# A two-block transformer kernel in split fp32: joint products taken out of ga to co, rows of 2,304 bytes for the first activation buffer, and waits of TensorE for its own last product at four panels

## The reference, cut to what matters

```python
# first block
a = rms_norm(h, norm_mix)
qkv = a @ w_qkv                                  # 2048 x 6144, then stick-breaking attention (16 heads)
h = h + o @ w_o                                  # 2048 x 2048
h = h + square(relu(rms_norm(h, norm_mlp) @ w1)) @ w2   # 2048 x 8192, 8192 x 2048
h = rms_norm(h, final_norm)
# second block: 16 meta tokens stand ahead of the 256 tokens
hn = rms_norm_2(h, norm_mix_g)
u, gb_in, gc_in, v_in, ga_lin, gbr_lin = split(hn @ w_in)          # 2048 x 12288
y_a = pool(u) @ pool_w * pool_scale              # trailing means over 2, 4, 8, 16 tokens
y_b = (gb_in * causal_conv3(gc_in * v_in)) @ conv_out_w
h = h + (sigmoid(ga) * y_a + sigmoid(gbr) * y_b) @ w_o2
h = h + (silu(hn2 @ w_gate) * (hn2 @ w_up)) @ w_down               # 2048 x 11264, 5632 x 2048
out = rms_norm_2(h, norm_final_g)[:, 16:]
```

## Time and profile before

| | |
|---|---|
| Three runs | 2572.61, 2572.88 (median), 2573.26 us |
| The profiled execution | 2572.07 us, span of its instructions 2570.3 us, granted clock 0.999 |
| PE busy | 2561.2 us (100%), 19,871 matmuls |
| PEld busy | 2461.8 us (96%) |
| DVE, ACT, POOL busy | 1578.9, 1153.0, 139.1 us (61%, 45%, 5%) |
| DMA | 485.64 MB, mean 189 GB/s, 56.8% of 16 engines |

### The profile page before, as it was taken

How to read it: one execution, slowest core, us unless ns; L and a number is a source line. 1 busy time by engine, 2 the same in 40 slices (tenths; PEclk the granted TensorE clock), 3 DMA queues, 4 the chain that set the end, 5 groups by cost and what they waited for, 6 DMA issues and landing times.

```text
span 2570.3 us, 47399 instructions
## 1 busy us (share of the span) xinstructions
PE 2561.2 (100%) x19871; PEld 2461.8 (96%) x19871; DVE 1578.9 (61%) x1343; ACT 1153.0 (45%) x1126; POOL 139.1 (5%) x87
## 2 busy tenths in 40 slices
PE   9999999999999999999999999999999999999998
PEld 9999999999999999999899988899999889998997
DVE  6577766655556556786654776566755555555555
ACT  5455554434434434544533344444444434443444
POOL 0000100000000000000200530000000000000001
PEclk9999999999999999999999999999999999999999
DMA  7554455556555565555555555555555556555563
GB/s 263 184 165 163 164 181 188 192 195 196 195 190 191 195 197 196 186 181 189 183 186 188 183 181 195 182 195 197 193 187 193 182 195 197 196 190 190 194 212 131
DMA packets 243978, 485.64 MB, mean 189 GB/s; under 512 B 7729, under 2 KB 8945, under 8 KB 243697
## 3 DMA queue, kind: packets, MB, share of 16 engines
q1 hardware_dynamic: 243520, 483.12, 56.8%
q10 hardware_dynamic: 320, 0.53, 0.1%
HBM read 481.53 MB, written 2.10 MB: 188 GB/s over the span
## 4 chain that ended last, share of the span: by engine, by line
PE 99%; DVE 0%; POOL 0%; issue 0%; ACT 0%; DVEq 0%; POOLq 0%; ACTq 0%
PE ps L1414 48%; PE ps L1422 24%; PE ps L1385 8%; PE ps L1347 8%; PE ps L1391 4%; PE ps L1357 4%; PE ps L1470 0%; PE ps L1524 0%; PE ps L1436 0%; PE ps L1458 0%; PE ps L1407 0%; PE ps L1278 0%; PE ps L1288 0%; PE ps L1529 0%; PE ps L1507 0%; PE ps L1461 0%
## 5 line engine op out<-in xcount | busy, mean ns | idle before, releaser
L790 DVE TENSOR_TENSOR wlo<-raw,whi 128x1024 fp32r<-128x1024 f32 x900 | 1138.9, 1274 | 944.1 <-ACT whi L582 943.8
L582 ACT ACTIVATE whi<-raw 128x1024 fp32r<-128x1024 f32 x900 | 949.9, 1060 | 1335.9 <-PE ps L1422 1008.4
L1414 PE MATMUL ps<-b_buf,whi 128*128 128x256 f32 x5734 | 711.5, 276 | 0.5 <-DVE za L1005 0.5
L1414 PEld LDWEIGHTS ps<-b_buf,whi 128*128 128x128 f32 x5734 | 679.6, 188 | 1.1 <-DVE za L1005 0.7
L1422 PE MATMUL ps<-b_buf,wlo 128*128 128x256 f32 x2880 | 386.3, 276 | 0.0
L1422 PEld LDWEIGHTS ps<-b_buf,wlo 128*128 128x128 f32 x2880 | 354.4, 188 | 0.0
L1414 PE MATMUL ps<-a_buf,whi 128*128 128x258 f32 (+4 forms) x2560 | 330.9, 282 | 0.0
L1414 PEld LDWEIGHTS ps<-a_buf,whi 128*128 128x128 f32 x2560 | 315.7, 188 | 0.3
L1414 PE MATMUL ps<-c_buf,whi 128*128 128x256 f32 x2542 | 314.4, 276 | 0.0
L1414 PEld LDWEIGHTS ps<-c_buf,whi 128*128 128x128 f32 x2542 | 300.4, 188 | 0.2
L1347 PE MATMUL ps<-a_buf,whi 128*128 128x512 f32 x768 | 185.7, 394 | 0.0
(11 more groups left out here) (206 smaller groups left out, 1254.4 us busy)
## 6 DMA issues: line engine op xcount, KB each, us to landing
raw<-in_mlp_w_dram SPq DMA_DIRECT2D x128, 1024.0 KB, 5.4
raw<-in_w_in_dram SPq DMA_DIRECT2D x96, 1024.0 KB, 5.1
raw<-in_w_gate_up_dram SPq DMA_DIRECT2D x88, 1024.0 KB, 5.0
raw<-in_sb_w_qkv_dram SPq DMA_DIRECT2D x44, 1024.0 KB, 5.1
raw<-in_w_down_dram SPq DMA_DIRECT2D x44, 1024.0 KB, 5.0
raw<-in_sb_w_o_dram SPq DMA_DIRECT2D x16, 1024.0 KB, 5.0
raw<-in_conv_out_w_dram SPq DMA_DIRECT2D x16, 1024.0 KB, 5.0
raw<-in_w_o_dram SPq DMA_DIRECT2D x16, 1024.0 KB, 5.0
```

Of the source, the lines that this page charges most:

```text
L582: act.activation(whi[:, unit_of(n, u)], raw[:, n % RAW, u * UK:(u + 1) * UK, :], ACT.Copy).then_inc(w_hi, 1)
L790: dve.tensor_tensor(wlo[:, s], raw[:, n % RAW, u * UK:(u + 1) * UK, :], cast(whi[:, s]), ALU.subtract).then_inc(w_lo, 1)
L1414: pe.matmul(outs[j], whi[:, s, kt, j * P:(j + 1) * P], part[:, x, tok], start=first and kt == 0 and part is hi and (alone or j % 2 == 0), ...
```

## The change

- An A row becomes 576 columns (2,304 bytes): 16 meta, 256 tokens high, 256 tokens low, the meta tokens' low part in reversed order, 32 unused. High and low tokens of a tile now lie 1,024 bytes apart. `ms` moves into space that is free at the time.
- `paired_chunk` and `RUNS` go; ga, gb, gbr and co run through `chunk`, 192 products of 256 columns a panel. ga and gb are written out as four panels.
- `Panel` has `joint`, a number of joint products for each chunk, and `settle`, by which PE waits before the panel's first product until its own last product has counted `w_used`. Four panels have both, with 5 joint products in chunk 0: q's and w_o's panel 2, ga's and gb's panel 0. In w1_0 the 4 and 5 are replaced by 5 in chunk 3 of panel 0 (behind the norm), in gu_0_first by 5 in chunk 3 of the gate panel; gu_1_first and gu_2_first keep their 4.
- A panel with joint products uses one bank for each j also in q and w_o. There are now 8 such panels where there were 19.
- In the wide kinds the low product takes the low tokens and the reversed meta columns and writes 16 columns further on (`lows`); DVE's evacuation first copies those few columns and adds them where they belong (2 more steps, for 12 panels).

```diff
+ROW = 2 * TW + 32
...
+SETTLED = dict(joint={0: 5}, settle=True)
...
-    add("q", 1, [Panel("q", "w_qkv", 0, lambda i, g=g: g * PW, src="A") for g in range(4)], ("q",))
+    add("q", 1, [Panel("q", "w_qkv", 0, lambda i, g=g: g * PW, src="A", **(SETTLED if g == 2 else {}))
+                   for g in range(4)], ("q",))
...
-            add("w1_0", 1, [Panel("relu2", "w1", 0, lambda i, g=g: g * PW, src="C", needs="w_o", pairs=(4, 5, 0, 0)[g])
+            add("w1_0", 1, [Panel("relu2", "w1", 0, lambda i, g=g: g * PW, src="C", needs="w_o", joint={3: 5} if g == 0 else None)
...
-    loop2("ga", "ga", "w_in", 4 * D, "A", pairs=RUNS)
+    add("ga", 1, [Panel("ga", "w_in", 0, lambda i, g=g: 4 * D + g * PW, src="A", **(SETTLED if g == 0 else {}))
+                  for g in range(4)], ("ga",))
...
-    loop2("gb", "gb", "w_in", 1 * D, "A", pairs=RUNS)
-    loop2("gbr", "gbr", "w_in", 5 * D, "A", pairs=RUNS)
-    add("co", 1, [Panel("co", "conv_out_w", 0, lambda i, g=g: g * PW, src="B", needs="gb", pairs=RUNS if g < 2 else 0)
-                  for g in range(4)], ("co",))
+    add("gb", 1, [Panel("gb", "w_in", 0, lambda i, g=g: 1 * D + g * PW, src="A", **(SETTLED if g == 0 else {}))
+                  for g in range(4)], ("gb",))
+    loop2("gbr", "gbr", "w_in", 5 * D, "A")
+    loop2("co", "co", "conv_out_w", 0, "B", "gb")
...
-        a_buf, a_off = place("a_buf", [P, 2, NT, TW], F32R)
+        a_buf, a_off = place("a_buf", [P, NT, ROW], F32R)
...
+        a_hi, a_lo, b_hi, b_lo = a_buf[:, :, 0:TW], a_buf[:, :, T:2 * TW], b_buf[:, 0], b_buf[:, 1]
+        m_lo = a_buf[:, :, TW + T:2 * TW][:, :, ::-1]
+        a_pair = a_buf[:, :, M:M + 2 * T].rearrange("p t (a n) -> p a t n", a=2)
...
+                if kind in WIDE:
+                    spare = M - WIDE[kind]
+                    step(dve.tensor_copy(S2[:, :, 0:spare], ps[:, 4 * half:4 * half + 4, TW:TW + spare][:, :, ::-1]))
+                    early = ps[:, 4 * half:4 * half + 4, WIDE[kind]:M]
+                    step(dve.tensor_tensor(early, early, S2[:, :, 0:spare], ALU.add))
...
+                if p.settle and c == 0:
+                    pe.wait_ge(w_used, cnt.at("chunk") * UNITS)
...
+                        joint = products[:p.joint.get(c, 0)] if u == 0 else []
...
+                        for part, dst, cols in ((x_hi_, outs, tok), (x_lo_, lows, low_tok)):
```

More of the change, by code:

```diff
@@ L98, with __init__ @@
 class Panel:
-    def __init__(self, kind, weight, row0, col, chunks=CH, tile0=0, src=None, needs=None, pairs=0):
+    def __init__(self, kind, weight, row0, col, chunks=CH, tile0=0, src=None, needs=None, joint=None, settle=False):
         self.kind, self.weight, self.row0, self.col = kind, weight, row0, col
         self.chunks, self.tile0, self.src, self.needs = chunks, tile0, src, needs
-        self.pairs = pairs
+        self.joint, self.settle = joint or {}, settle
+        self.four = kind in FOUR or bool(joint)
     def counts(self):
-        more = TWO_PARTS if self.pairs else {}
+        more = TWO_PARTS if self.joint else {}
         return {k: KINDS[self.kind].get(k, 0) + more.get(k, 0) for k in NAMES}
@@ L209, in make_stages @@
     ready["kv"] = o_ready
-    add("w_o", 1, [Panel("res", "w_o1", 0, lambda i, g=g: g * PW, src="B", needs="kv") for g in range(4)], ("res",))
+    add("w_o", 1, [Panel("res", "w_o1", 0, lambda i, g=g: g * PW, src="B", needs="kv", **(SETTLED if g == 2 else {}))
+                     for g in range(4)], ("res",))
     stages[-1].order = ([(0, 0), (0, 1), (0, 2), (1, 0), (1, 1), (1, 2), (0, 3), (1, 3)] +
@@ L251, in make_stages @@
     for f, n in enumerate((4, 4, 3)):
-        ready[f"gu_{f}"] = (gate_up(f"gu_{f}_first", done, 1, norm=None if f else 2, pairs=(4, 0) if f else (0, 5)) +
+        ready[f"gu_{f}"] = (gate_up(f"gu_{f}_first", done, 1, norm=None if f else 2, joint={0: 4} if f else {3: 5}) +
                             gate_up(f"gu_{f}_rest", done + 1, n - 1, j0=1))
@@ L308, in build @@
         rr1, _ = place("rr1", [P, T])
-        ms, _ = place("ms", [P, 2, TW])
         msum = rr[:, 0:M]
@@ L641, in evac @@
             def evac(p, j):
-                kind, two = p.kind, int(bool(p.pairs))
+                kind, two = p.kind, int(bool(p.joint))
                 dst = {"q": tiles(b_hi, j), "k": k_hi[:], "v": v_hi[:], "res": tiles(c_hi, j),
@@ L1331, in three @@
                 return pe.matmul(out, w_l, x_h, start=False, stop=stop, skip_group_check=True)
[L1333 to L1344, removed]
-                    if back == 0 and kt == 0 and j == 0:
-                        pe.wait_ge(w_hi, cnt.at("chunk") * UNITS + (u + 1))
-                    high = pe.matmul(ps[:, 4 * half + j, :].rearrange("p (a n) -> p a n", a=2),
-                                     whi[:, unit_of(n - back, u), kt, j * P:(j + 1) * P],
-                                     buf[:, :, p.tile0 + (c - back) * KT + u * UK + kt, tok],
-                                     start=i < JT, stop=False, skip_group_check=True)
-                    if back and i % PER_RUN == PER_RUN - 1:
-                        high.then_inc(w_used, 1)
-                for u in range(UNITS):
-                    pe.wait_ge(w_lo, cnt.at("chunk") * UNITS + (u + 1))
-                    for kt in range(UK):
-                        for j in range(JT):
-                            last = pe.matmul(ps[:, 4 * half + j, T:2 * T], wlo[:, unit_of(n, u), kt, j * P:(j + 1) * P],
-                                             buf[:, 0, p.tile0 + c * KT + u * UK + kt, tok], start=False,
-                                             stop=c == p.chunks - 1 and u == UNITS - 1 and kt == UK - 1,
-                                             skip_group_check=True)
-                    if u < UNITS - 1 or end == (c + 1) * PER_RUN:
-                        last.then_inc(w_used, 1)
-                cnt.n["chunk"] += 1
             def chunk(p, c, half):
```

64 lines of the change are left out of this document (29 added, 35 removed).

## The result

Four runs of the changed kernel took 2618.49 to 2619.26 us (median 2618.70), beside 2573.01 for the kernel before: ratio 1.0178 [1.0160, 1.0196]. Forecast were 2559.2 us and a gain of 0.5%; it is 1.8% slower. The profiled execution took 2618.55 us.

What follows compares the result with a forecast made beforehand. PE, busy for the whole span, was taken to bound the kernel. Gains of 13.49 us, settling +1.32 and -0.5, -0.6, -0.4 gave -13.7 from 2572.07; with 0.8 added, 2559.2 us, range 2550 to 2565.

Steps and rivals of the forecast that it cites:

- Two paces that a stream keeps: On PE, 256-column products run at 113.3 or 117.8 ns (21.76 or 22.62 us a panel), and the stream keeps its pace.
- rival 3: The switch to the short pace at gb's start misses, costing 14.4 us up to gu_0's norm; 2573.6 us, chance 0.03.
- The row starts (9 x 256 bytes): A's rows stepping by 9 x 256 bytes look constant to PE, so A holds the short pace as B and C do.
- Rival 4: A cannot hold the short pace, shown by 279 to 283 ns in ga; +9.1 us, 2582 us, chance 0.08.
- five joint products are shown to work from the long pace: Five 512-column products at q, w_o, ga, gb and behind two norms switch PE to the short pace, costing 0.02 us a time.
- A door without a price: Moving joint products behind the norms in w1_0 and gu_0 gains 0.22 us each; no cost of a miss was given.
- rival 2: The switch to the short pace misses at one of q, w_o or ga; 2561.5 to 2563.4 us, chance 0.10.
- Settling: PE's wait for its own last product at q, w_o, ga and gb costs 0.33 us each, 1.32 in all.
- pw: pw's panels go from 22.94 to 21.76 us, gaining 1.18, of which 0.48 is the stall; 0 to 0.5 may return.
- Wide panels: The 258-column products of gc, vv and u stay near today's time on constant rows; -0.5 us taken.
- v: v's first two chunks gain 0.19 us and its other 14 chunks 0 to 1.3, taken as -0.6.
- Rival 5: The pace hangs on neither row starts nor joint products; only split products and settling count, 2578 us, chance 0.02.

Runs made afterwards that it cites:

- experiment 8: Experiment 5 with w1_0's panel 1 and gu_0's up panel entered by 5 joint products without a wait; 2563.91 us, ratio 0.9966.
- experiment 5: Changed kernel with wait plus 4 joint products at q, w_o, gb, w1_0's panel 1 and gu_0's up panel, wait plus 6 at ga; 2597.49 us.
- experiment 6: Experiment 5 with A's rows of 2,176 bytes instead of 2,304; 2615.56 us, ratio 1.0166.
- experiment 4: Changed kernel with the wait kept but no joint products at q, w_o, ga and gb; 2586.48 us, ratio 1.0059.
- experiment 1: Changed kernel with 4 joint products instead of 5 at q, w_o, ga, gb and behind the norms in w1_0 and gu_0; 2583.75 us, ratio 1.0057.
- experiment 9: Experiment 5 with the change's own 5 joint products behind the norms, in place of wait plus 4, in w1_0 and gu_0; 2596.70 us.
- experiment 10: Experiment 5 with 7 joint products instead of 4 at w1_0's panel 1 and 6 at gu_0's up panel, wait kept; 2597.62 us.

## Why the prediction was wrong

**What bounds it, the clock:** right. Nothing but the pace moved more than some 3 us.

**Two paces that a stream keeps:** right, in size as well. The kernel before kept the short one for 674 us, where I had written 640. The eighth experiment's panels take 21.76 us on every stretch that I had named but pw, with 0.1 more in those behind a wait. My price for a miss at gb's door (rival 3, 13.8 us for its 16 panels) measured 13.6 in the change against the forecast (gb and gbr 2.3 + 4.55 - 0.33, the wait's gap ahead of them 0.26, co 2.75 + 0.67, wo2 3.4).

**The row starts (9 x 256 bytes):** right: A holds the short pace in experiments 5 and 8 and loses it in 6. Rival 4, the slower end on which I had put 0.08, is not what happened: A's products showed 279 in ga, which I had named as its sign, but so did B's and C's, and the sign could not tell the rivals apart.

**The step that failed** is the reading of the earlier trace rows: "a few 512-column products ... throw it over", and from that "five joint products are shown to work from the long pace", wherever they stand. What the earlier trace rows shows is one sequence of five, behind single products at the long pace, that ended on 232. Behind a wait the first distance is 313, behind a norm 421; the sequence is shifted, and the fifth falls on 226 or 229. I read one success as a property of the number five. The rows that would have warned me were at hand: the kernel before used 4, 5, 5, 4 and 4, and each of the five sequences ends on 231 or 232.

**A door without a price.** For w1_0 and gu_0 I took 0.22 us each as the whole stake, since the change only moves five joint products from one chunk to the one before. That move puts the norm just ahead of them, and what hangs on them is everything up to the next door: 31 panels x 0.855 = 26.5 us, and 7 panels, 6 us. I priced misses at q, w_o, ga and gb, and not at these two, which made more than half of the error. With a price on them the slower end would have stood at 2592 (both missed), or 2606 with gb's as well. The misses were also not independent, as the chances of rivals 2 and 3 took them: six of six missed, each shifted in the round. Only rival 2's remark that five may throw wrong what the wait has set right touched it, and experiment 4 shows that the wait alone sets nothing right at these four.

**The sum, term by term** (against the forecast of 2558.4 for the profiled execution, 60.2 us): w1_0 to w2_3 27.2, gu_0 with dn_0 6.8, gb to wo2 13.6, ga 3.4, q with k 2.5, w_o 1.9, pw 0.6, v 1.9, wide panels 1.2; together 59.1, the rest in the first panels and between attention's parts. A wait's gap lies in the stretch ahead of its door (0.26 in u for ga's, 0.26 in vv for gb's) and is counted here with the door.
- **Settling**, 0.33 each: in experiment 8 the first panel behind the wait takes 21.86 us instead of 21.76 in q, with about 0.26 of gap ahead of it (380 ns where 118 would stand): 0.36. At w_o, where the last distance is 539, it is 0.5. Right but for w_o.
- **pw**: 22.94 to 22.32, not 21.76; the stall shrank to 0.02 as forecast, and the pace stayed long up to its third panel. In experiment 8, where PE comes sooner, 0.24 of the stall is back (a distance of 356), inside my 0 to 0.5, but it also costs the short pace for two panels (0.43): 22.53 in all. From one stall I had read that a stall throws the stream to the short pace; this one throws it the other way.
- **Wide panels**, -0.5 forecast: gc and vv +0.9 in the change and in experiment 8 (184.15 and 184.16 against 183.25), u +0.3 in both. Without the gaps of the waits it is +0.6 and nothing. Their products' middle duration in gc and vv is unchanged:
```profile
L1394 PE MATMUL ps<-a_buf,whi x1024: 277/282/285, 1334.4 to 1517.2; 128*128 128x258 f32 x171
```
- **v**, -0.6 - 0.19 forecast, the wrong sign: with activations stationary, L1363's products in A take 397 ns in the mean, against 394; the four v panels grew by 1.1 us:
```profile
L1363 PE MATMUL ps<-whi,a_buf 128*128 128x512 f32 x256 | 65.2, 397 | 0.0
```

So the plan, with the doors of experiment 8, was worth 2573 - 2564 = 9 us, not 13.7; between that and the forecast stand wide panels and v (about 3), pw (0.8), the pace behind attention's parts (0.5) and several terms of 0.2: the chunks behind the two norms, w_o's wait.

**Rival 5**, that row starts and joint products set no pace (2578 us), is not what happened: experiment 6 (18 us for 128 bytes a row) and experiment 1 (35 us between the medians for one product fewer at six places) speak against it. The Trainium skill (page "TensorE: Matmul & The Clock Gate", "Step-by-step: what each phase is for") says that weights load through a port of their own and take nothing from the running matmul. These runs contradict what I had drawn from that sentence, that row starts would not matter; whether weight loads take anything they do not show.

**What stays open.** What in PE or its weight loads makes the two paces was not shown. In the trace a weight load of 187 to 188 ns starts 2 to 4 ns behind each product's start at either pace, so these rows don't say which of the two sets it. That the number of joint products decides at one place, and that what works goes with the last distance within a few nanoseconds, is shown; whether that distance is the cause or only a mark of where the stream stands is not, nor why 306 230 236 232 misses and 236 235 232 232 hits. And of experiment 1 only the execution at 2598.92 was traced: which doors fell otherwise in the runs at 2583 and 2608 is not known.

## What to carry to other kernels

Where a dense stream of matmuls can run at two paces, read the pace of every stage (duration of one product, start to start), before and after, even of stages that the change doesn't touch, and price each place that sets the pace by all that runs up to the next such place. A recipe that works in one spot, a count of instructions above all, is a fact of that spot and its entry: when anything ahead of it moves, look at the start-to-start distances there again and choose the count anew. A stall is such a place too: pw's led to either pace. Here other counts at four doors and two doors moved back turned a loss of 1.8% into a gain of 0.34%.

## What the runs showed of the hardware

- Two to seven fp32r products of 512 columns fall into a round of 226, 229, 232 ns between their starts, and their place in it bears on the pace of what follows: all 55 doors that gave the short pace (113.3 ns for 256 columns) ended on a duration of 394 or 395 (24 of them the same two places in twelve kernels), and none of the 29 that ended on another did. Six with 394 did not either.
- In the kernel before the pace then held over 31 panels and 674 us, across changes of buffer and of PSUM banks, up to the first wide product.
- A moving operand whose rows start 2,304 bytes apart holds 276 ns; at 2,176 bytes it wanders over 276 to 284 (18 us in the whole kernel, 2615.56 against 2597.49, of it 6.8 in stages on other buffers that inherit the pace). B's and C's 1,024 hold it as well.
- A wait of PE for its own last product costs 0.36 us here, 0.5 where the distance ahead was 539, and did not by itself change the pace at any of four places entered at the long one. pw's stall of 0.24 us, entered at the short pace, was followed by the long one in all four kernels that had it (experiments 5, 8, 9, 10).
